# Combining each token's two expert rows: first row written with its residual, second row added

## The reference, cut to what matters

```python
n = rms_norm(x, norm_ffn)
out[t] = sum over the 2 experts e of t: gate[t, e] * ((silu(n[t] @ w_gate[e]) * (n[t] @ w_up[e])) @ w_down[e])
y = x + out
```

## Time and profile before

| | |
|---|---|
| time, median of 3 runs | 1089.93 us (1089.51 to 1091.01) |
| time of the profiled execution | 1091.88 us |
| its span, first to last instruction | 1090.1 us |
| busy PE, DVE, ACT, GpSimd | 1045.2, 544.4, 309.3, 174.6 us |
| moved by DMA | 293.19 MB, 269 GB/s over the span |
| landing of a scatter, median | 9.1 us |

### The profile page before, as it was taken

One profiled execution on the slowest core, in us unless ns is written; L12 is line 12 of the kernel. 1 busy time (PEld: TensorE's weight loads), 2 busy tenths in 40 slices (PEclk: granted clock), 3 DMA queues, 4 the chain that ended last, 5 costly groups with the idle time before them and its releaser, 6 DMA issues.

```text
span 1090.1 us, 29226 instructions
## 1 busy us (share of the span) xinstructions
PE 1045.2 (96%) x12774; PEld 826.0 (76%) x12774; DVE 544.4 (50%) x1052; ACT 309.3 (28%) x592; POOL 174.6 (16%) x160
## 2 busy tenths in 40 slices
PE   8999999999999999999999999999999988898996
PEld 7999999966666549899876898756898556565665
DVE  5327654378875543444734544555455534343431
ACT  6323332266775552222411011101110111101011
POOL 1001200599200000100010111111111111111102
PEclk9999999999999999999989999999999999999999
DMA  7356785000116467767899999999999999999994
GB/s 244 109 166 211 217 272 155 1 13 2 40 31 211 146 232 251 245 220 277 312 351 393 379 383 385 386 383 375 386 379 382 379 390 388 392 390 389 390 389 111
DMA packets 85816, 293.19 MB, mean 269 GB/s; under 512 B 13425, under 2 KB 44849, under 8 KB 60069
## 3 DMA queue, kind: packets, MB, share of 16 engines
q1 hardware_dynamic: 78277, 273.30, 67.2%
q0 software_dynamic: 7280, 17.58, 6.8%
q10 hardware_dynamic: 128, 0.39, 0.1%
HBM read 272.98 MB, written 42.87 MB: 290 GB/s over the span
## 4 chain that ended last, share of the span: by engine, by line
PE 73%; DMA 18%; DVE 4%; SPq 2%; ACT 1%; issue 1%; POOL 0%; ACTq 0%; POOLq 0%
PE bank L2827 20%; DMA w_all<-in_w_up 18%; PE bank L2375 12%; PE bank L2612 8%; PE bank L2418 4%; PE bank L2844 4%; PE bank L2584 3%; PE bank L2547 3%; PE bank L2848 3%; PE bank L2456 3%; SPq L1042 2%; PE bank L2852 2%; DVE keep L1887 1%; PE bank L2693 1%; PE bank L2479 1%
## 5 line engine op out<-in xcount | busy, mean ns | idle before, releaser
L2827 PE MATMUL bank<-w_all,xeT 128*32 128x256 f32 x6144 | 345.6, 382 | 22.2 <-DMA w_all<-in_w_up 19.2
L2827 PEld LDWEIGHTS bank<-w_all,xeT 128*32 128x32 f32 x6144 | 254.4, 111 | 107.0 <-issue 27.9
L2202 DVE STREAM_TRANSPOSE xeT<-xg 32x256 f32<-32x256 f32 x360 | 156.5, 435 | 97.0 <-DMA xg<-n_scr,tab 91.8
L2844 PE MATMUL bank<-w_all,hT 128*32 128x256 f32 x744 | 165.6, 379 | 0.0
L2848 PE MATMUL bank<-w_all,hT 128*32 128x512 f32 x744 | 129.3, 592 | 0.0
L1887 DVE TENSOR_TENSOR_SCAN keep<-keep,unseen 128x1024 f32<-128x1024 f32 (+7 forms) x64 | 94.8, 1514 | 37.8 <-ACT keep L1439 37.7
L2375 PE MATMUL bank<-w_hi,xh 128*128 128x256 f32 x376 | 108.1, 287 | 0.0
L2375 PE MATMUL bank<-w_hi,xl 128*128 128x256 f32 x376 | 105.5, 281 | 0.0
L2375 PE MATMUL bank<-w_lo,xh 128*128 128x256 f32 x376 | 105.5, 280 | 0.0
L2844 PEld LDWEIGHTS bank<-w_all,hT 128*32 128x32 f32 x744 | 81.8, 110 | 30.3
L1681 ACT ACTIVATE sgl<-bank 128x384 f32<-128x384 f32 x32 | 15.7, 490 | 304.2 <-PE bank L2827 304.2
(11 more groups left out here) (307 smaller groups left out, 1505.9 us busy)
## 6 DMA issues: line engine op xcount, KB each, us to landing
w_all<-in_w_down SPq DMA_DIRECT2D x64, 1024.0 KB, 30.2
w_all<-in_w_gate SPq DMA_DIRECT2D x64, 1024.0 KB, 32.6
w_all<-in_w_up SPq DMA_DIRECT2D x64, 1024.0 KB, 8.9
k_scr<-in_cache_k SPq DMA_DIRECT2D x32, 256.0 KB, 3.3
v_scr<-in_cache_v SPq DMA_DIRECT2D x32, 256.0 KB, 3.5
pgk<-k_scr SPq DMA_DIRECT2D x32, 256.0 KB, 3.9
w_raw<-in_w_in SPq DMA_DIRECT2D x7, 1024.0 KB, 7.1
pgv<-v_scr SPq DMA_DIRECT2D x4, 1024.0 KB, 6.6
```

The costliest lines, as they stand in the source:

```text
L2202: last = dve.transpose(xeT[i][rows_of(s), :, rows_of(g)], lane[:, :, s, :])
L2827: lasts = [pe.matmul(pair_ps(i)[rows_of(q), g, :, :], xeT[i][:, k, rows_of(g)], pair_of(b, i, k, q), start=(k == 0 and g != 1), stop=(k == ...
L2844: return pe.matmul(y_right_ps(g), hT[:, ft, rows_of(g)], w[ft // 2][:, ft % 2, DA:D], start=first and g != 1, stop=ends, skip_group_check= ...
```

## The change

Rows in `n_scr` no longer carry the norm's gain, only the division by the root, so a gathered row times the root gives the token's x back. The router makes one more table, `wtab`: the root for a slot whose expert is the first of the token's two in the order of the blocks, zero for the other. ACT writes gathered row times `wtab` into `yo` (`keep_rows`), which takes the place of left_rows; DVE adds the gated product to it (`add_rows`, five instructions, in place of right_rows' two). Two indirect DMAs then scatter `yo`: the adding one to the rows that are a token's second (`tab_later`), and behind it a plain one to the rows that are its first (`tab_first`); the slots of the other kind are out of bounds in each. Together they move the same rows as the one before. The gain is put on after the transpose, by eight activations per block on ACT (`gains`). Gathers go a block further ahead: gather(b+4) follows moved(b) and waits for keep_rows(b+2), the other reader of its buffer. The order of experts is changed so that a token's first expert always comes before its second. The first store of xmid to `y_all` stays. The last block (two half scatters) adds as before.

```diff
     rhs, prod, tmp32, ek, le = table(at_tmp, at_yo_end, (
-        ("rhs", [P, 2, NB, 2 * NE], F32), ("prod", [P, 2, NB, NE], F32),
+        ("rhs", [P, 2, NB, 3 * NE], F32), ("prod", [P, 2, NB, NE], F32),
...
-    tab_ps = bank[0:CAP, 7, 0:2 * NE]
+    tab_ps = bank[0:CAP, 7, 0:3 * NE]
...
-    expert_of = list(range(NE))
-    expert_of[NE - 1 - EPG], expert_of[NE - 1] = NE - 1, NE - 1 - EPG
+    expert_of = [e for e in range(NE) if e != NE - 1 - EPG] + [NE - 1 - EPG]
...
-        return 16 * (b + 1) if type(b) is int and b < NE - 1 else 16 * (b + 2)
+        return 32 * (b + 1) if type(b) is int and b < NE else 16 * (b + NE + 1)
...
@@ GpSimd
             def gather(b):
...
                 if b >= 2:
                     pool.wait_ge(s_xt if b < 4 else s_xc, b - 1)
+                if 2 <= b < NE:
+                    pool.wait_ge(s_ya, b - 1)
...
             def scatter(b):
...
-                                        out_offset=bass.IndirectOffsetOnAxis(ap=rows_named(b, sidx), axis=0),
+                                        out_offset=bass.IndirectOffsetOnAxis(
+                                            ap=column(tab_later, b) if b < NE else sidx[b % 2][:, 0:1].bitcast(U32), axis=0),
                                         in_=yo[b % 2][:, :], in_offset=None, compute_op=ALU.add,
                                         bounds_check=T - 1, oob_is_err=False).then_inc(s_sc, 16)
+                if b < NE:
+                    pool.indirect_dma_start(out=y_all,
+                                            out_offset=bass.IndirectOffsetOnAxis(ap=column(tab_first, b), axis=0),
+                                            in_=yo[b % 2][:, :], in_offset=None,
+                                            bounds_check=T - 1, oob_is_err=False).then_inc(s_sc, 16)
...
-            pool.tensor_tensor(xg[0][0:r, :].rearrange("r (k p) -> r p k", p=P)[:, P // 2:P, :], xs, gs, ALU.mult).then_inc(s_lrg, 1)
...
-            gather(2)
+            for b in range(2, 4):
+                gather(b)
...
             for b in range(NE - 1):
-                if b + 3 < NE:
-                    gather(b + 3)
                 scatter(b)
                 if b < NE - 2:
                     moved(b)
+                if b + 4 < NE:
+                    gather(b + 4)
@@ ACT
-                act.activation(xeT[i][:, 0:KT // 2, :], xT_ps[:, 0:KT // 2, 0:CAP], ACT.Copy).then_inc(s_xe, 1)
+                for k in range(KT // 2):
+                    last = act.activation(xeT[i][:, k, :], xT_ps[:, k, 0:CAP], ACT.Copy, scale=gain_p[:, k:k + 1])
+                last.then_inc(s_xe, 1)
+
+            def gains(b, i):
+
+                act.wait_ge(s_xc, b + 1)
+                for k in range(KT):
+                    last = act.activation(xeT[i][:, k, :], xeT[i][:, k, :], ACT.Copy, scale=gain_p[:, k:k + 1])
+                last.then_inc(s_xe, 1)
+
+            def keep_rows(b, i):
+
+                act.wait_ge(s_gl[i], 16 * (b // 2 + 1))
+                if b < 2:
+                    act.wait_ge(s_tab, 1)
+                else:
+                    act.wait_ge(s_sc, scatters(b - 2))
+                act.activation(yo[i][:, :].rearrange("r (p k) -> r p k", p=P), xg[i][0:CAP, :].rearrange("r (k p) -> r p k", p=P),
+                               ACT.Copy, scale=wtab[:, expert_of[b]:expert_of[b] + 1]).then_inc(s_ya, 1)
...
             def first_act():
                 for b in range(2):
                     block_left(b, b)
+                for b in range(2):
+                    keep_rows(b, b)
                 silu(0, 0)
+                gains(2, 0)
 
             def block_act(i, b):
                 silu(b + 1, 1 - i)
-                left_rows(b, i)
+                if b + 3 < NE:
+                    gains(b + 3, 1 - i)
+                if b + 2 < NE - 1:
+                    keep_rows(b + 2, i)
@@ DVE
+            def name_residuals(q):
...
+                chain.link(dve.tensor_tensor(places, oh[:, :, ts, :], numbers, ALU.mult))
+                chain.link(dve.reduce_sum(turn[:, :, ts], places, axis=AXX))
+                for k in range(2):
+                    chain.done(dve.tensor_tensor(weight[:, k, ts], turn[:, k, ts], turn[:, 1 - k, ts], ALU.is_lt))
+                chain.settle()
+                chain.link(dve.tensor_tensor(weight[:, :, ts], weight[:, :, ts],
+                                             sig[:, ts].rearrange("p (x t) -> p x t", x=1).to_broadcast([P, 2, n]), ALU.mult))
+                return dve.tensor_tensor(residual_table(q), ek[:, :, 0:n, :], each(weight[:, :, ts], NE), ALU.mult)
...
-                dve.scalar_tensor_tensor(out=xg[t % 2][0:r, :].rearrange("r (k p) -> r p k", p=P), in0=rows[0],
-                                         scalar=rs[0:r, c], in1=rows[1], op0=ALU.mult, op1=ALU.mult).then_inc(s_n2, 1)
+                dve.tensor_scalar(xg[t % 2][0:r, :].rearrange("r (k p) -> r p k", p=P),
+                                  xmid[0:r, t, :].rearrange("r (p k) -> r p k", p=P), rs[0:r, c], None, ALU.mult).then_inc(s_n2, 1)
...
+            def result_tables():
+
+                dve.wait_ge(s_tbp, 5)
+                chain.done(dve.tensor_copy(gtab[:, 0:NE], tab_ps[:, NE:2 * NE]))
+                chain.link(dve.tensor_copy(wtab[:, :], tab_ps[:, 2 * NE:3 * NE]))
...
+            def add_rows(b, i):
+                dve.wait_ge(s_dp, 8 * b + 8)
+                dve.wait_ge(s_ya, b + 1)
+                gates = gates_of(b, i)
+
+                def add(rows, cols, product):
+                    out = yo[i][rows, cols]
+                    return dve.scalar_tensor_tensor(out=out, in0=product, scalar=gates[rows, :], in1=out, op0=ALU.mult, op1=ALU.add)
+
+                add(slice(0, CAP), slice(0, 512), y_left_ps)
+                add(slice(0, CAP), slice(512, DA), y_mid_ps)
+                for g in range(LANES):
+                    last = add(rows_of(g), slice(DA, D), y_right_ps(g))
+                last.then_inc(s_yd, 1)
...
             def first_dve():
                 for b in range(2):
                     block_right(b, b)
+                result_tables()
                 count_overflow()
...
             def block_dve(i, b):
                 hidden(b + 1, 1 - i)
-                right_rows(b, i)
+                add_rows(b, i)
                 turn_hidden(b + 1)
@@ PE
             last_tables(slice(NE, 2 * NE))
-            keep_warm(14)
+            keep_warm(8)
+            pe.wait_ge(s_gn, 3)
+            residual_tables()
+            keep_warm(4)
```

More of the change, by code:

```diff
@@ L327, in slot_tables, with residual_table @@
         return late_oh[:, :, at:at + n, :], late_rhs[:, :, at:at + n, :]
+    late_res, turn, weight = table(at_b, at_b + 1120, (
+        ("late_res", [P, 2, NB, NE], F32), ("turn", [P, 2, NT], F32), ("weight", [P, 2, NT], F32)))
+    def residual_table(q):
+        if q == 2:
+            return late_res[:, :, :, :]
+        return rhs[:, :, 0:BATCHES[q][1] - BATCHES[q][0], 2 * NE:3 * NE]
     before, ones, io_row = table(at_masks, at_u, (
@@ L732, in last_lane_ps @@
         return bank[CAP:P, 2 + part, (DH - DQ) * g:(DH - DQ) * (g + 1)]
-    expert_of = list(range(NE))
-    expert_of[NE - 1 - EPG], expert_of[NE - 1] = NE - 1, NE - 1 - EPG
+    expert_of = [e for e in range(NE) if e != NE - 1 - EPG] + [NE - 1 - EPG]
+    assert all(sorted(g) == g for g in ([e for e in expert_of if e // EPG == n] for n in range(NGRP)))
     assert expert_of[NE - 1] // EPG != expert_of[NE - 2] // EPG
     def scatters(b):
-        return 16 * (b + 1) if type(b) is int and b < NE - 1 else 16 * (b + 2)
+        return 32 * (b + 1) if type(b) is int and b < NE else 16 * (b + NE + 1)
     def copies(b):
-        return scatters(b) // 16 if type(b) is int else b + 2
+        return b + 1 if type(b) is int and b < NE - 1 else b + 2
     parts = []
@@ L1662, in _ @@
             act.wait_ge(s_ssq2, NT)
-            act.activation(rs[0:r, 0:1], ss[0:r, 0:1], ACT.Sqrt, bias=rest, scale=1.0 / D).then_inc(s_rms2, 1)
+            act.activation(sig[0:r, LAST:NT], ss[0:r, 0:1], ACT.Sqrt, bias=rest, scale=1.0 / D).then_inc(s_rms2, 1)
             act.dma_start(y_all[row0(LAST):T, :], xmid[0:ROWS[LAST], LAST, :]).then_inc(s_yl, 16)
@@ L1714, in last_act @@
                     silu(b + 1, 1)
-                    left_rows(b, 0)
                 else:
@@ L2146, in _ @@
                         chain.done(name_gates(q))
+                        chain.done(name_residuals(q))
                         name_rows(q)
@@ L2197, in turn_rows @@
                 dve.wait_ge(s_gp, 8 * b - 8)
-                dve.wait_ge(s_xe, b)
                 for g in range(LANES):
@@ L2268, in last_dve @@
                     turn_hidden(b + 1)
-                    right_rows(b, 0)
+                    add_rows(b, 0)
                 else:
@@ L2751, in last_tables, with residual_tables @@
                 last.then_inc(s_tbp, 1)
+            def residual_tables():
+                lo, hi = BATCHES[2]
+                one_hot = slot_tables(2)[0]
```

(6 more changed lines are left out.)

81 lines of the change are left out of this document (39 added, 42 removed).

## The result

| | before | changed | ratio (95% interval) |
|---|---|---|---|
| median, us (lowest to highest, 4 runs each) | 1090.47 (1089.51 to 1093.62) | 1148.04 (1143.99 to 1151.48) | 1.0521 (1.0473 to 1.0570) |
| profiled execution: span, us | 1090.1 | 1149.0 | |

The change makes the kernel slower by 57.6 us. Forecast were 1136 us and a range of 1110 to 1168.

What follows compares the result with a forecast made beforehand. PE's 15.54 us a block up to 828 us, then the DMA's pace, were taken as bounds. Block 4 late by 10.6, the steps to block 31 +33.1 and the tail +2.6 gave +46.3: 1136 us, range 1110 to 1168.

Steps and rivals of the forecast that it cites:

- the two old limits: Expert stage before the change: PE at 15.54 us a block up to 828 us, then the DMA's loading of w_up.
- The DMA's gain: Block scatters: 34 of 67 rows become plain, saving 0.0075 us each, 0.25 a block, 7.9 us over 31 blocks.
- Circle 1: Loop of gather, transposes, gains, keep_rows, next gather, one block per turn: 19.5 us with full queues, 14.9 with light ones.
- Circle 2: Loop of row additions, scatter pair, keep_rows, silu, hidden product, next row additions: 18.1 us, 17.3 with the cheap keep_rows.
- The relief: In the expert loop: if the DMA runs dry, the gather lands up to 4.6 us sooner.
- The pace of 18.1: Expert loop: us a block, taken between the DMA's 17.6 and the gather loop's 19.5; 24 steps at it.
- The last steps: Last three steps to block 31: load queues are empty, so they go at PE's 15.6 us each.
- The start: Ahead of the loop: block 2 starts 5.9 us late, block 4 at 623.1 instead of 612.52, 10.6 late.
- The tail: After the last blocks: longer row additions and four scatters instead of three in GpSimd's queue, +2.6 us.
- (a): Rival: the loop gets no relief, 19.2 us a step, 1162 us, up to 1170; chance 0.22.
- (b): Rival: the DMA's new pace rules, 17.2 to 17.6 us a block, 1114 to 1124; 0.62 together with the forecast.
- (c): Rival: both loops come under 16.3 us a block and vanish behind PE and DMA, 1084.6 us; chance 0.08.

Runs made afterwards that it cites:

- e7: v2 with keep_rows, from block 2 on, scaling the result buffer in place instead of reading gathered rows, leaving those blocks' residual out: 1087.71 us.
- e8: The kernel before with its block scatters as plain writes instead of adding ones, except in the last block: 1074.67 us.
- e4: The changed kernel with one adding scatter of the whole block in place of the pair: 1139.84 us.
- e2: The changed kernel with a block's eight gain multiplications moved from ACT to one DVE product behind the transposes: 1135.23 us.
- e6: The changed kernel with a block's row additions put ahead of the next block's hidden product on DVE: 1136.68 us.
- e1: The changed kernel with keep_rows reading and writing in plain order, so residual columns come out permuted: 1130.60 us.
- v4: v2 with the normalised rows stored so that keep_rows reads in order and DVE's transposes read with a stride: 1125.94 us.
- v2: The changed kernel with the edits of e2 and e6 together: 1110.95 us.
- v1: The changed kernel with keep_rows moved from ACT to GpSimd and e2's edit as well: 1137.71 us.
- e3: The changed kernel with keep_rows moved from ACT to GpSimd, gains staying on ACT: 1139.25 us.
- e5: The changed kernel with a block's two scatters in the other order, the plain one first: 1145.26 us.

## Why the prediction was right

**What bounds the kernel** held: the two old limits vanish together in the changed kernel, and come back in e7 when the circles are taken away (step 16.06, w_up as the releaser). PE was to be busy 85 to 88% and is 90%; the DMA was to move 379 GB/s and moves 369 to 372, for the pace is slower.

**The DMA's gain** held. 0.25 us a block or 7.9 us were said; e7 shows 8.8 at block 31, e8 confirms that an adding row costs more than a plain one. In the changed kernel nothing of it can be seen in the time, since the DMA no longer sets it. The second DMA and its empty packets were priced at nothing. Queue 0 bears that out: it takes 79.7 us of all engines in e4 (7.0% of 1139.2) and 70.1 in the changed kernel (6.1% of 1149.0), 9.7 less, where half of e8's 21.6 would be 10.8; so the 3472 further packets cost some 1 us in all, within the rounding of the shares.

**Circle 1**, 19.5 us with full queues: 20.2 in the turn from 696.95 to 717.14 (gather to transposes 9.66 and not 8.3, transposes 5.37, gains 2.23 and not 2.75, keep_rows 2.10 and not 1.95, 0.89 to the gather). The gains were too dear by 0.5: one takes 362 ns by its own row, but eight in a row follow each other every 0.28 us. The gather was too cheap for this turn by 1.4; over the loop its mean is 7.5.

**Circle 2**, 18.1: 18.13 in the turn shown, additions 2.61 and not 2.7, the pair 11.34 from issue to keep_rows and not 11.0. e2 shows it alone at 18.28, as e6 shows circle 1 alone at 18.25, and only both edits together bring the step down, to 17.39.

**keep_rows** at 1.95 with the stride or 1.15 without: 2.14 and 1.14 (e1). The rule of the Trainium skill ("SBUF — State Buffer", section on the DMA port swizzle) is that elements more than 16 bytes apart pay at each access; this case's rows agree, with 2.14 against 1.14 us on ACT, and with 642 against 435 ns for DVE's transposes in v4. By how much they pay only the rows say.

**The relief** is real: 7.5 us on the mean from gather to transposes, against 8.8 in the kernel before. It isn't steady as was thought. From block 15 to 27 a long and a short landing alternate (8.3 to 9.9 and 5.1 to 6.5 us). It looks like an equilibrium: e1 and v2 shortened the loop and got 0.5 of 1.0 and 1.1 of 2.4 us a step, with later landings. The pace of 18.1, chosen between 17.6 and 19.5, was a little low: 18.44 from block 4 to block 28. **This is the term that was mis-sized**: these 24 steps take 442.5 us (1064.33 - 621.79) and not 434.4, 8.1 more.

**The last steps** were to go at PE's 15.6 from block 28 on. Only the last did (15.51): the step from block 28 to 29 was still a circle's (18.30), and the next (17.24) lost 1.7 us to a gate-and-up product of 12.25 us, with a granted clock of 0.86 over it. From block 28 to 31 are 51.05 us and not 46.8. The two errors make 12.4 us; with the start 1.3 earlier and the tail 1.6 longer than said they give the 12.6 by which the sum of 46.3 fell short of 58.9.

**The start** seems to hold, block 2 at 586.92 (587.4 said), block 4 at 621.79 (623.1), but that is in part luck. The sum was reckoned from the kernel before, whose granted clock from 540 to 560 us is 0.83; the changed kernel's profiled run had 0.66 there. With that clock goes the issue of gather(2): 570.55 here and 570.12 in v1 (0.66), 567.66 in e3 and 567.39 in e7 (0.83), 567.00 in e5 (0.91), 563.9 to 564.7 in e1, e2, e6 and v2 (1.00). The sum had 570.8. In e5 the first pair of scatters was also no longer awaited 7.1 us after its issue, where it took 11.0 here, and block 4 starts at 615.42, only 2.9 us late and not 9.3. So the start's 10.6 is near the dear end of what one run can show. **The tail** is 4.2 and not 2.6.

**The rivals.** (a), no relief, is out by the mean landing of 7.5 us and the step of 18.44, not 19.2, though the median of 1148 is only 2 us below its range; (b), the DMA's pace, by a share of 0.97 with PE idle; (c) needed landings of 5.1 us, and the formula of the Trainium skill ("DMA: Bandwidth & Descriptors", section on the anatomy of one DMA on the GpSimd path) makes it an estimate of 2.7 us for the gather. The trace differs, and decides: 5.1 to 9.9 inside the loop, and 3.5 and 3.7 in the last two turns (issued at 1086.01 and 1100.15 us), where the DMA share has fallen to 0.20 and 0.24. The estimate is near only where the queues are almost empty. What happens at (c)'s point is seen in e7: no circle, 1087.71 us, not far above its 1084.6.

**What stays open.** That longer landings made v2 fall short was read from its timeline, not tested apart. How much of the 57.6 us is the start in the median run is not known, since only one run of each kernel was profiled. A version with a real third pair of buffers, which would do what e7 does without leaving the residual out, was not built. By e7 it could win 2.4 us. No version that does the whole work beat the kernel before; v2 is the best of those with this change.

## What to carry to other kernels

A buffer that gets a second reader ties two engines' orders together: follow the new wait round until it comes back, and count how many blocks one round advances. Two circles of the same length must be opened in one experiment, since each alone shows only a third of the gain in time, and a fifth in the step. Two profiled runs should be compared by stretches: the clock ahead of the loop alone moved a start by several us here. What a faster DMA is worth must first be weighed against the rest of the kernel: the plain rows were worth 8.8 us on the stream in e7, 4.4 of which went in the tail; in the changed kernel the start took 9.3 us, the loop 45.5 and the tail 4.2.

## What the runs showed of the hardware

- Landings of indirect DMAs take longer where the queues carry more: from a gather's issue to its use 3.5 us at a DMA share of 0.20, 7.5 on the mean at 371 GB/s (changed kernel), 8.3 at 385 (e1), 9.0 at 389 (v2), 8.8 at 390 (e7); from the pair's issue to keep_rows 11.2 us on the mean of the ten turns that waited for it in the changed kernel, 11.3 at 381 GB/s (e2), 12.4 at 389 (v2).
- A VectorE product of 128x768 takes 0.96 us in e7 and 1.57 in v1, where GpSimd copies 96x1024 rows for 3.9 us a block. The groups of the two kernels, e7's first:

```profile
L2264 DVE TENSOR_TENSOR xeT<-xeT,gain_p 128x768 f32<-128x768 f32 x30 | 28.7, 958 | 1.0
```

```profile
L2270 DVE TENSOR_TENSOR xeT<-xeT,gain_p 128x768 f32<-128x768 f32 x30 | 47.0, 1566 | 1.0
```

- That the two engines hinder each other is the nearest reading; it was not tested apart.
- Twelve of the 28 gate-and-up products from block 4 on took 11.8 to 13.5 us and not 10.6, each behind a wait of PE of 2.4 to 6.3 us; three others behind waits of 2.3 to 3.6 us took 10.6. Over the product of block 4 the granted clock is 0.86, over that of block 5 1.00: part of the long one ran at 1.2 and not at 2.4 GHz. It costs little, as PE isn't on either circle: from 560 us on silu waits for PE once and the row additions twice. It counted in the last steps.
- The page's count of bytes written to memory rises from 42.87 to 55.06 MB, 12.19 MB or 31 x 96 x 4096 bytes, though the queue moved 17.60 MB as before: as if each of the two scatters were counted with all its 96 rows. e4, with one scatter, has 42.87 again. It's no measure of traffic here.
